# Convolution stage of a two-block network kernel: four of fourteen weight chunks multiplied as plain float32 products

## The reference, cut to what matters

```python
z = _rmsnorm(h, mix_norm[i]) @ w_in[i]                     # 256 x 1024 times 1024 x 2576
conv_a, conv_gt, q, k, v, r, g_lr = jnp.split(z, SPLIT_POINTS, axis=-1)
y_conv = _conv_module(conv_a, conv_gt, ...)                # 31 taps over time, LayerNorm, silu
y_gla = _gla(q, k, v, r, g_lr, ...)                        # gated linear attention, times silu(r)
h = h + jnp.concatenate([y_conv, y_gla], axis=-1) @ w_out[i]
```

## Time and profile before

| | before |
|---|---|
| median of 3 runs | 1617.9 us (1615.13 to 1618.08) |
| the profiled execution, its own time | 1618.3 us |
| its span in the trace | 1616.5 us |
| PE busy | 1567.8 us, 97% |
| DVE busy | 1100.2 us, 68% |
| ACT busy | 740.3 us, 46% |
| DMA moved | 341.08 MB, mean 211 GB/s |

### The profile page before, as it was taken

How to read it: one execution, slowest core, us unless ns; L and a number is a source line. 1 busy time by engine, 2 the same in 40 slices (tenths; PEclk the granted TensorE clock), 3 DMA queues, 4 the chain that set the end, 5 groups by cost and what they waited for, 6 DMA issues and landing times.

```text
span 1616.5 us, 30500 instructions
## 1 busy us (share of the span) xinstructions
PE 1567.8 (97%) x12582; PEld 1528.9 (95%) x12582; DVE 1100.2 (68%) x1325; ACT 740.3 (46%) x823; POOL 13.0 (1%) x33
## 2 busy tenths in 40 slices
PE   6999999899999999999999899999999999999998
PEld 6999998689999999999998799999999999999998
DVE  4777779956777767777767677777744456754444
ACT  5433354454333473333567553334533345453333
POOL 2000000000000000000000000000000000000000
PEclk8999999799999999999999999999999999999999
DMA  6988844238878549888453388886455554555551
GB/s 213 347 304 285 286 150 150 91 125 281 291 269 301 183 132 309 281 300 293 140 172 101 97 289 299 293 286 219 157 182 182 182 156 156 169 167 182 185 181 53
DMA packets 244682, 341.08 MB, mean 211 GB/s; under 512 B 5891, under 2 KB 188315, under 8 KB 244624
## 3 DMA queue, kind: packets, MB, share of 16 engines
q1 hardware_dynamic: 242656, 334.72, 61.8%
q0 software_dynamic: 1968, 5.54, 1.0%
HBM read 339.17 MB, written 2.63 MB: 211 GB/s over the span
## 4 chain that ended last, share of the span: by engine, by line
PE 90%; DVE 5%; ACT 4%; DMA 1%; issue 1%; SPq 0%; DVEq 0%; ACTq 0%
PE bank L1322 28%; PE bank L1324 28%; PE bank L1323 28%; PE bank L1449 2%; ACT w_hi L447 1%; DVE w_lo L825 1%; DVE arena L1041 1%; PE bank L1394 1%; ACT L467 1%; ACT xn L458 1%; DVE xn L977 1%; DMA raw<-in_ffn_w_in 1%; DVE x_res L994 0%; PE bank L1383 0%; PE bank L1661 0%
## 5 line engine op out<-in xcount | busy, mean ns | idle before, releaser
L1322 PE MATMUL bank<-xs_hi,w_hi 128*128 128x256 f32 x2496 | 713.5, 286 | 12.1 <-DVE xs_lo L831 9.1
L1323 PE MATMUL bank<-xs_lo,w_hi 128*128 128x256 f32 x2496 | 708.1, 284 | 0.0
L1324 PE MATMUL bank<-xs_hi,w_lo 128*128 128x256 f32 x2496 | 707.9, 284 | 0.0
L825 DVE TENSOR_TENSOR w_lo<-raw,w_hi 128x2048 fp32r<-128x2048 f32 x245 | 560.4, 2289 | 215.0 <-ACT w_hi L447 206.1
L447 ACT ACTIVATE w_hi<-raw 128x2048 fp32r<-128x2048 f32 x245 | 466.5, 1906 | 236.0 <-PE bank L1324 219.1
L1322 PEld LDWEIGHTS bank<-xs_hi,w_hi 128*128 128x128 f32 x2496 | 480.8, 193 | 20.0 <-issue 19.4
L1323 PEld LDWEIGHTS bank<-xs_lo,w_hi 128*128 128x128 f32 x2496 | 481.1, 193 | 1.0 <-issue 1.0
L1324 PEld LDWEIGHTS bank<-xs_hi,w_lo 128*128 128x128 f32 x2496 | 480.9, 193 | 0.0
L1322 PE MATMUL bank<-gu_hi,w_hi 128*128 128x256 f32 x960 | 274.6, 286 | 0.0
L1324 PE MATMUL bank<-gu_hi,w_lo 128*128 128x256 f32 x960 | 271.7, 283 | 0.0
L1323 PE MATMUL bank<-gu_lo,w_hi 128*128 128x256 f32 x960 | 271.5, 283 | 0.0
(11 more groups left out here) (235 smaller groups left out, 1220.1 us busy)
## 6 DMA issues: line engine op xcount, KB each, us to landing
ada<-in_ada_w SPq DMA_DIRECT2D x72, 1024.0 KB, 5.9
raw<-in_ffn_w_in SPq DMA_DIRECT2D x44, 1024.0 KB, 7.0
raw<-in_ffn_wg SPq DMA_DIRECT2D x44, 1024.0 KB, 6.0
raw<-in_ffn_wu SPq DMA_DIRECT2D x44, 1024.0 KB, 5.4
raw<-in_ffn_wd SPq DMA_DIRECT2D x44, 1024.0 KB, 5.0
raw<-in_ffn_w_out SPq DMA_DIRECT2D x22, 1024.0 KB, 6.6
raw<-in_attn_w_qkv SPq DMA_DIRECT2D x12, 1024.0 KB, 5.1
raw<-in_w_in SPq DMA_DIRECT2D x10, 1024.0 KB, 5.3
```

Of the source, the lines that this page charges most:

```text
L825: dve.tensor_tensor(w_lo[:, s, :], raw[:, s, :], w_hi[:, s, :].bitcast(F32), ALU.subtract)\
L1322: pe.matmul(out_, a_hi, b_hi, start=start, stop=False, skip_group_check=True)
L1323: pe.matmul(out_, a_hi, b_lo, start=False, stop=False, skip_group_check=True)
L1324: return pe.matmul(out_, a_lo, b_hi, start=False, stop=stop, skip_group_check=True)
```

## The change

Chunks 6 to 9 (values and output gate) get no high and low parts. PE multiplies the raw float32 weights with the full activations `xn` in one plain float32 matmul per tile and column group: 16 instructions of 256 columns per chunk in the program. ACT and DVE leave these four chunks out. Since the raw slot is now read by PE itself, the loads that overwrite chunks 6 to 9, which are those of chunks 9 to 12, wait for the product (`chunks_done`) in the place of the low part. Counts of high and low parts are shifted by `nth_split`.

```diff
+UNSPLIT = [BASE[1] + j for j in range(6, 10)]
+
+def nth_split(c):
+    return c + 1 - sum(u <= c for u in UNSPLIT)
...
             def load(c, src, i=0):
                 s = c % SLOTS
-                if c >= SLOTS:
-                    sp.wait_ge(lo_ready, c - SLOTS + 1 + 3 * i)
+                if c - SLOTS in UNSPLIT:
+                    sp.wait_ge(chunks_done, c - SLOTS + 1)
+                elif c >= SLOTS:
+                    sp.wait_ge(lo_ready, nth_split(c - SLOTS) + 3 * i)
...
             def split(c, s=None):          # ACT, and the same in DVE's
                 looped = s is not None
-                if not looped and c >= TOTAL:
+                if not looped and (c >= TOTAL or c in UNSPLIT):
                     return
...
+            def wide_plain(s, b, t):
+                w = lin(s, raw)
+                for nb in range(2):
+                    for k in range(KT):
+                        ins = pe.matmul(bank[b][:, nb * T:(nb + 1) * T], w[:, k, nb * P:(nb + 1) * P], t[:, k, :],
+                                        start=(k == 0 and nb == 0), stop=(k == KT - 1), skip_group_check=True)
+                ins.then_inc(chunks_done, 1)
+
+            def token_major_plain(s, b):
+                w = lin(s, raw)
+                for k in range(KT):
+                    for t in range(2):
+                        ins = pe.matmul(bank[b][:, t * NC:(t + 1) * NC], xn[:, k, t * P:(t + 1) * P], w[:, k, :],
+                                        start=(k == 0 and t == 0), stop=(k == KT - 1), skip_group_check=True)
+                ins.then_inc(chunks_done, 1)
...
                 for j in range(10):
-                    arrived(c + j)
+                    if c + j in UNSPLIT:
+                        pe.wait_ge(raw_in[(c + j) % SLOTS], 16 * ((c + j) // SLOTS + 1))
+                    else:
+                        arrived(c + j)
                     if j in (6, 7):
                         pe.wait_ge(ev("glu_done"), 1)
-                        token_major((c + j) % SLOTS, j - 6)
+                        (token_major_plain if c + j in UNSPLIT else token_major)((c + j) % SLOTS, j - 6)
+                    elif c + j in UNSPLIT:
+                        if j in (8, 9):
+                            pe.wait_ge(ev("glu_done"), 2)
+                        wide_plain((c + j) % SLOTS, (1, 0, 3, 2, 4, 5, None, None, 2, 3)[j], xn)
```

More of the change, by code:

```diff
@@ L817, in split @@
                 looped = s is not None
-                if not looped and c >= TOTAL:
+                if not looped and (c >= TOTAL or c in UNSPLIT):
                     return
                 if looped:
-                    dve.wait_ge(hi_ready, c[0] + 1 + 3 * c[1])
+                    dve.wait_ge(hi_ready, nth_split(c[0]) + 3 * c[1])
                 else:
                     s = c % SLOTS
-                    dve.wait_ge(hi_ready, c + 1)
+                    dve.wait_ge(hi_ready, nth_split(c))
                 dve.tensor_tensor(w_lo[:, s, :], raw[:, s, :], w_hi[:, s, :].bitcast(F32), ALU.subtract)\
@@ L1326, in arrived @@
             def arrived(c, i=0):
-                pe.wait_ge(lo_ready, c + 1 + 3 * i)
+                pe.wait_ge(lo_ready, nth_split(c) + 3 * i)
             def wide(s, b, hi, lo, each=None):
```

## The result

The changed kernel takes 1622.26 us (median of 6 runs, 1620.6 to 1624.79), the one before 1617.76 us (6 runs, 1615.13 to 1618.08). The ratio is 1.0034, 95% interval 1.0022 to 1.0046. So the change costs 4.5 us by the medians, 5.5 us by the ratio and 3.6 to 7.4 us by the interval: slower. The forecast was +5.1 us.

The account below looks back on a forecast made before the run. PE's matmuls bound the whole kernel; the stage ends a fixed time after chunk 12's low part. Product +0.55, load +5.0 and silu beside the load -0.5 gave +5.1 us, 1623.0 us against the median; range 1619.3 to 1626.8.

Parts of the forecast that it names:

- What bounds the stage: On DVE, the last 36 convolution steps follow chunk 12's low part, so the stage ends a fixed time after it.
- The freed 9.2 us turn into waiting: DVE loses four low parts, 9.2 us, but then stands waiting before `log_a`.
- The price of a plain product: On PE, 0.2155 us per record, 6.90 us per chunk, +1.14 us per chunk against the split product.
- both bounds: Plain product on PE: 5.76 us per chunk below (sum +0.5), 7.7 us above (sum +8.2).
- Product 9, +0.5 to +0.6: On PE, dearer products less removed waiting and slow matmuls end product 9 later by +0.5 to +0.6 us.
- the term of 1.1 us for the slow stretch: On PE, the first 12 matmuls of product 8 no longer run at reduced clock, saving 1.1 us.
- The loads, +5.0: Loads of chunks 10 to 12 start only when products 7 to 9 end and land 5.0 us after issue.
- What follows moves along: After chunk 12's low part, `ke_t`, `kv`, selection, states and 36 steps keep their order and move by 5.1 us.
- the rival of a clock that returns later: At the stage's tail, full clock returns one stretch later than before: +3.3 us, 1626.3; chance 7%.
- The rival of a clock that takes it back: At the stage's tail, full clock returns before the convolution ends, regaining 3.0 us: +2.1, 1620.0; chance 10%.
- Plain products cheaper than three or dearer: Two rivals on PE: cheaper, 3.8 us per chunk, -5.6, 1612.3, 4%; dearer, +8.2, 1626.1, 6%.
- Loads hidden: The loads hide by an unseen path, leaving only product 9's own delay: +0.6 us, 1618.5; chance 7%.

Follow-up runs that it names:

- conv_early: spare_buffer with 20 of DVE's last 36 convolution steps moved ahead of `log_a`; 1615.96 us, ratio 0.9998 to the kernel before.
- late_12: The kernel before, all products split in three, only the load of chunk 12 waiting for product 9; 1620.09 us, ratio 1.0028.
- late_loads: The kernel before, all products split, loads of chunks 9 to 12 waiting for the product three chunks earlier; 1623.96 us, ratio 1.0045.
- spare_buffer: The changed kernel with chunk 9 landing in idle buffer `ub`, so loads of 10 to 12 wait for products 6 to 8; 1617.29 us, ratio 1.0005.
- only_9: The changed kernel with only chunk 9 multiplied plainly, 6 to 8 split as before; 1618.35 us, ratio 1.0014 to the kernel before.
- hold_13: The changed kernel with the load of chunk 13 held until the low part of chunk 12; one execution, 1620.59 us.
- only_9_spare: only_9 with chunk 9 landing in buffer `ub`, so that no load waits for a product; 1613.46 us, ratio 0.9979.
- changed_again: The changed kernel unaltered, run once more for its trace (the second profile); one execution, 1620.41 us.
- two_plain: The changed kernel with only chunks 8 and 9 plain, 8 in `ub`, chunk 12's parts behind the states, convolution steps moved; 1610.29 us, ratio 0.9963.

## Why the prediction was right, point by point

- **What bounds the stage.** The stage ends a fixed time after the low part of chunk 12. In the changed kernel that is +5.7 us at the low part (+5.4 in the second profile) and +5.7 at the start of the normed outputs (324.34 - 250.43 = 73.91 against 68.21). Right.
- **The freed 9.2 us turn into waiting.** Right, 8.55 us in front of `log_a`. conv_early shows how little they would have been worth even if filled.
- **The price of a plain product.** 0.2155 us per record was read from matmuls with a tile of ones, 0.216 was measured. Right; both bounds, 5.76 and 7.7 us per chunk, are out. The four passes of the Trainium skill ("FP8 and Floating Point Precision", section TensorE Precision Notes) do not come as four split matmuls of 0.12: a plain matmul is two records of 0.216, 0.43 us in all. The trace disagrees with that reading, not with the count of passes, which no run here shows.
- **Product 9, +0.5 to +0.6.** Measured +0.59. (The sum as it is written, +4.56 - 2.4 - 0.4 - 1.1, gives +0.66; the times chunk by chunk give +0.5.) Of this sum the term of 1.1 us for the slow stretch is not a property of the kernel before: late_12 had the same 2.2 us of idle PE and no slow stretch. Against an execution in which it does not fall, the changed kernel would lose 1.1 to 1.5 us more by this sum; that was not run as a pair. In the profile of before it did, so the sum against that profile held; in that the term was lucky, since nothing in the prediction says why the stretch should fall in each execution.
- **The loads, +5.0.** The term that decides. late_loads and late_12 show it alone, spare_buffer shows the change without it. It was 5.0 to 5.6 us and not always 5.0: with 5.6 in the first profile and 5.4 in the second the low part of chunk 12 came 5.7 and 5.4 us later, not 5.1. The Trainium skill's fit ("DMA: Bandwidth & Descriptors", section Anatomy of one DMA), from which the prediction took its estimate of 4.4 us, is given there for DMAs that GpSimd issues. These loads are issued by SP, and no load of chunk 12 behind product 9 took less than 5.0 us.
- **What follows moves along.** Nearly. In the first profile the granted clock was 0.56 over 325 to 330 us and 0.75 over 330 to 335 (before: 0.94 and 1.00), and the stage was 6.7 us longer at its end; in the second (0.71 and 1.00) it was 5.3. So the rival of a clock that returns later was there once, worth 1.0 us and not 3.3. The rival of a clock that takes it back was not: in the second profile the end differs by 0.1 us from what the low part says, and so it does in every other run where that low part stands on the path (late_loads, late_12, spare_buffer, only_9, hold_13, only_9_spare).
- **The number.** +4.5 us by the medians and +5.5 by the ratio lie around the +5.1, but an interval of 3.6 to 7.4 us cannot tell terms of half a microsecond apart. The terms are shown by the timings of the stage, not by the times of the kernels.
- **The rivals.** Plain products cheaper than three or dearer: out by the row. Loads hidden: out by the DMA on the chain. "Product 9's own delay alone is left if the loads are free" (+0.6, 1618.5) is what spare_buffer measured: +1.0 us by the medians, +0.4 at the end of the stage.

## What to carry to other kernels

Before you let a later engine read a buffer directly, ask who gets the buffer next, and when. Here the raw slot was free after the low part, with a whole product's time in hand, and now only after the product, and each following load landed 5.1 to 5.6 us after that product had ended. The last of them cost its full 5 us. One spare buffer took the cost away, to within what these runs can tell. And time freed on an engine that works in a fixed order is worth something only as far as there is work behind the next wait that may go in front of it; move that work, and then look for the next path.

## What the runs showed of the hardware that had not been expected

- **The same idle time of PE does not always cost the clock.** In the profile of before PE was idle 2.25 us and the next 12 matmuls stood 0.21 us apart; in late_12 it was idle 2.24 us and they stood 0.12 apart. The granted clock over 280 to 285 us was 0.66 in the one, with the 1.2 GHz level at its start, and 1.00 in the other, 2.4 GHz throughout. This is worth 1.1 us by the sum, and may be a part of the spread between executions; that was not tested.
- **The landing of a 1 MB load scatters by 0.6 us.** The load of chunk 12, issued behind product 9 with no other load ahead of it, took 5.6 us in the changed kernel, 5.4 in changed_again, 5.2 in hold_13 and 5.05 to 5.07 in late_12, only_9, late_loads and two_plain, without regard to what was issued behind it.
